# Splitting attention queries on their token rows and transposing once per head

## The reference

```python
def odd_mixer_latent(h, kc, vc, w_qkv, w_out, sink):
    q, k, v = split_qkv(h, w_qkv)          # 16 query heads of 64, 4 key/value heads
    q = rope_2d(q)
    k = rope_2d(k)
    return latent_attention(q, k, v, kc, vc, sink) @ w_out
...
    s_loc = jnp.einsum('bnqkgd,bnmkd->bnkgqm', qb, kw).astype(jnp.float32) * scale
    s_ctx = jnp.einsum('bnqkgd,bskd->bnkgqs', qb, kc).astype(jnp.float32) * scale
    p = jax.nn.softmax(jnp.concatenate([s_loc, s_ctx, sk], axis=-1), axis=-1)
```

## Time and profile before

| | us |
|---|---|
| median of three runs | 1598.37 |
| lowest and highest run | 1596.35, 1603.43 |
| profiled execution, its own time | 1597.03 |
| its span on the core | 1595.1 |
| TensorE busy | 1487.3 |
| VectorE busy | 667.9 |
| ScalarE busy | 545.9 |
| GpSimd busy | 508.8 |

### The profile page before, as it was taken

One profiled execution on the slowest core, in us unless ns is written; L12 is line 12 of the kernel. 1 busy time (PEld: TensorE's weight loads), 2 busy tenths in 40 slices (PEclk: granted clock), 3 DMA queues, 4 the chain that ended last, 5 costly groups with the idle time before them and its releaser, 6 DMA issues.

```text
span 1595.1 us, 20092 instructions
## 1 busy us (share of the span) xinstructions
PE 1487.3 (93%) x8338; PEld 1234.4 (77%) x8338; DVE 667.9 (42%) x1137; ACT 545.9 (34%) x904; POOL 508.8 (32%) x215
## 2 busy tenths in 40 slices
PE   4899889899999999999789889999799999999998
PEld 3776676688898899897567656657699889989985
DVE  4476763642222222233734566624532222223225
ACT  4376533631131232222531366515523113212311
POOL 1312133233143243232324234404333324332430
PEclk8999899999999999999999999999999999999999
DMA  9324145234343222134142000033332213212221
GB/s 343 126 80 132 60 130 180 67 121 158 124 139 113 73 84 75 55 104 157 45 172 80 27 1 2 1 107 131 99 100 80 76 57 101 64 61 93 80 84 75
DMA packets 90546, 153.87 MB, mean 96 GB/s; under 512 B 6404, under 2 KB 44752, under 8 KB 90456
## 3 DMA queue, kind: packets, MB, share of 16 engines
q1 hardware_dynamic: 82432, 145.76, 27.7%
q10 hardware_dynamic: 8024, 6.83, 1.5%
HBM read 149.69 MB, written 2.89 MB: 96 GB/s over the span
## 4 chain that ended last, share of the span: by engine, by line
PE 40%; DVE 3%; ACT 3%; DMA 2%; POOL 1%; issue 1%; ACTq 0%; DVEq 0%; SPq 0%
PE PS L1267 11%; PE PS L1268 11%; PE PS L1269 11%; PE PS L1556 2%; PE PS L1548 1%; POOL WL L927 1%; PE PS L1523 1%; PE PS L1506 1%; PE PS L1524 1%; DMA RAW<-in_w_ffn_in 1%; ACT WH L699 1%; DVE RAW L573 1%; PE PS L1319 1%; ACT RAW L573 1%; DMA RAW<-in_w_mod 0%
## 5 line engine op out<-in xcount | busy, mean ns | idle before, releaser
L927 POOL TENSOR_TENSOR WL<-RAW,WH 128x1024 fp32r<-128x1024 f32 x170 | 420.1, 2504 | 782.0 <-ACT WH L699 782.0
L1267 PE MATMUL PS<-HH,WH 128*128 128x384 f32 (+1 forms) x1152 | 359.6, 312 | 14.1 <-DVE HL L1080 7.9
L1268 PE MATMUL PS<-HL,WH 128*128 128x384 f32 (+1 forms) x1152 | 358.2, 311 | 0.0
L1269 PE MATMUL PS<-HH,WL 128*128 128x384 f32 (+1 forms) x1152 | 358.1, 311 | 0.0
L699 ACT CAST WH<-RAW 128x1024 fp32r<-128x1024 f32 x170 | 168.2, 1045 | 477.1 <-PE PS L1269 307.8
L1267 PE MATMUL PS<-WH,AH 128*128 128x512 f32 x640 | 251.4, 393 | 9.0 <-DVE ACC L1187 9.0
L1268 PE MATMUL PS<-WL,AH 128*128 128x512 f32 x640 | 250.1, 391 | 0.0
L1269 PE MATMUL PS<-WH,AL 128*128 128x512 f32 x640 | 250.0, 391 | 0.0
L1267 PEld LDWEIGHTS PS<-HH,WH 128*128 128x128 f32 x1152 | 221.1, 192 | 19.3 <-issue 10.2
L1268 PEld LDWEIGHTS PS<-HL,WH 128*128 128x128 f32 x1152 | 221.2, 192 | 0.6
L1269 PEld LDWEIGHTS PS<-HH,WL 128*128 128x128 f32 x1152 | 220.8, 192 | 0.0
(11 more groups left out here) (184 smaller groups left out, 1641.6 us busy)
## 6 DMA issues: line engine op xcount, KB each, us to landing
RAW<-in_w_mod SPq DMA_DIRECT2D x43, 1024.0 KB, 5.1
RAW<-in_w_ffn_in SPq DMA_DIRECT2D x32, 1024.0 KB, 5.7
RAW<-in_w_ffn_out SPq DMA_DIRECT2D x32, 1024.0 KB, 4.9
RAW<-in_w_in_even SPq DMA_DIRECT2D x7, 1024.0 KB, 5.5
RAW<-in_w_qkv SPq DMA_DIRECT2D x6, 1024.0 KB, 5.3
RAW<-in_w_out_even SPq DMA_DIRECT2D x4, 1024.0 KB, 5.1
RAW<-in_w_out_odd SPq DMA_DIRECT2D x4, 1024.0 KB, 6.2
X<-in_x_sample SPq DMA_DIRECT2D x4, 512.0 KB, 7.1
```

The costliest lines, as they stand in the source:

```text
L927: nc.gpsimd.tensor_tensor(ring_view(WL, ld, j), w_view(ld, b), ring_view(WH, ld, j).bitcast(f32), ALU.subtract).then_inc(w_lo, 1)
L1267: MM(out, wh, xh, start=first, stop=False)
L1268: MM(out, wh, xl, start=False, stop=False)
L1269: return MM(out, wl, xh, start=False, stop=last)
```

## The change

Before, TensorE makes both halves of `QS` by multiplying the query rows with the identity twice, into partitions 0 to 63 and 64 to 127 of a PSUM bank; ScalarE copies all of it, rounding; VectorE subtracts on the upper 64 partitions. After it, VectorE first makes rounded part and remainder side by side on the token rows, in one of two buffers (`Q2`, which share memory with `PART` and `BMR`), one unit ahead; TensorE transposes 128 columns per head at once, and ScalarE copies the bank to `QS` and frees it.

```diff
+        Q2B = alias("Q2B", [P, 512])
+        Q2 = [PART[:, :], Q2B[:, :]]
...
-                    nc.scalar.copy(QS[:, i % 2, :], m_bank(u)).then_inc(q_hi, 1)
+                    nc.scalar.copy(QS[:, i % 2, :], m_bank(u)).then_inc(m_free[u % 2], 1)
...
-            def query_remainder(i):
-
-                u = Q_M[i]
+            def query_split(i):
+
+                g, t = i % NKV, i // NKV
+                if i > 1:
+                    upto(dve, m_ready, Q_M[i - 2])
+                q = ACC[:, t, 256 * g:256 * g + 256].rearrange("p (h d) -> p h d", h=4)
+                hi, lo = (Q2[i % 2].rearrange("p (h w d) -> p h w d", h=4, w=2)[:, :, w, :] for w in (0, 1))
+                V_.tensor_copy(hi.bitcast(f32r), q).then_inc(q_hi, 1)
                 dve.wait_ge(q_hi, i + 1)
-                V_.tensor_tensor(QS[64:128, i % 2, :], m_bank(u)[64:128, :], QS[64:128, i % 2, :].bitcast(f32),
-                                 ALU.subtract).then_inc(m_free[u % 2], 1)
+                V_.tensor_tensor(lo, q, hi, ALU.subtract).then_inc(q_split, 1)
...
                 elif k == "Q":
                     if s["n"] == 0:
-                        query_remainder(0)
+                        upto(dve, b_free, QKV_B - LAT)
+                        query_split(0)
+                    if s["n"] + 1 == NKV:
+                        dve.wait_ge(qk_ready, 3 * LAT)
+                    if s["n"] < TT * NKV - 1:
+                        query_split(s["n"] + 1)
...
-                    if i + 1 < TT * NKV:
-                        query_remainder(i + 1)
...
                     m_acquire(u)
-                    if s["n"] == 0:
-                        upto(pe, b_free, QKV_B - LAT)
-                    if s["n"] == NKV:
-                        pe.wait_ge(qk_ready, 3 * LAT)
+                    pe.wait_ge(q_split, s["n"] + 1)
                     for h in range(4):
-                        c = HD * (4 * g + h)
-                        for half in (0, 64):
-                            ins = MM(m_bank(u)[half:half + 64, P * h:P * h + P], ACC[:, t, c:c + HD], IDN[:, :], start=True, stop=True)
+                        ins = TR(m_bank(u)[:, P * h:P * h + P], Q2[s["n"] % 2][:, P * h:P * h + P], IDN[:, :])
                     ins.then_inc(m_ready[u % 2], 1)
```

More of the change, by code:

```diff
@@ L475, in hybrid_step @@
         sum_ready = sem("sum_ready")
-        k_out, k_hi, q_hi = sem("k_out"), sem("k_hi"), sem("q_hi")
+        k_out, k_hi, q_hi, q_split = sem("k_out"), sem("k_hi"), sem("q_hi"), sem("q_split")
         qk_ready, v_done = sem("qk_ready"), sem("v_done")
```

## The result

| | before | after |
|---|---|---|
| median, us (4 runs each) | 1598.24 | 1588.84 |
| lowest and highest run | 1596.35, 1603.43 | 1587.29, 1591.47 |
| profiled execution, its own time | 1597.03 | 1587.29 |
| its span | 1595.1 | 1585.4 |

The ratio is 0.9932, with a 95% interval from 0.9912 to 0.9952: the changed kernel is 9.4 us faster by the medians. A second timing of the same kernel gave 0.9925 (0.9913 to 0.9937).

A forecast was written before the change was run, and what follows sets the result against it. TensorE was taken to set the pitch in the units of latent tiles. The terms 3.3 + 1.7 - 0.9 - 3.0 - 1.0 - 2.9 = -2.8 us took the median from 1598.37 to 1595.6 us, range 1590 to 1602.

The forecast's parts named there:

- The pair thus costs 0.38 + 0.69 + 0.08 ... = 1.15 us to 1.45 us: VectorE's new rounding copy and subtraction per unit, priced as 128x512 operations plus two hand-overs; 1.2 us taken.
- the first hole: At the first query, TensorE waits for VectorE's first split, so the projection goes on later: +3.3 us.
- units 7 to 11: Loop units where a GpSimd ring and the pair sticking out limit TensorE's saving: -1.0 us (0 to -2.15).
- The step falls from 1.02 to 0.59, by 0.43 us: TensorE's query step per unit: eight products of a 64-column weight tile become four transposes of 128 columns.
- units 12 to 18: TensorE-bound loop units with the pair covered: 7 x 0.43 less 0.1, -2.9 us.
- Units 2 to 6: Units 3 to 6, in a ring between ScalarE and VectorE, give -3.0 us; query 3 gives nothing.
- the remainder's place: VectorE's query remainder between sums and reduction, 0.72 us, goes away in units 3, 4, 5: 2.2 us.
- The ring of 7.64 us: Around unit 9, sums, GpSimd, small operations and exponentials form a cycle that an earlier reduction doesn't shorten.
- The half clock behind it: One stretch at granted clock 0.50 behind the first query's hole: +1.7 us (0 to 3.4).
- The saving without the stretch at the low clock: Rival: no low-clock stretch behind the first query's hole; sum -4.5, 1593.9 us; chance 0.22.
- VectorE does not become the bound: Denies the rival that a dear copy or GpSimd's hold-up makes VectorE the bound: +1.1, 1599.5 us; chance 0.20.
- The full promise: Rival: the whole 8.6 us saved on TensorE, first hole filled by something: about 1589.8 us; chance 0.07.

The follow-up runs named there:

- run 1: The kernel before with only TensorE's part: four full transposes of unsplit query rows for the eight identity products; 1589.64 us, ratio 0.9939.
- run 2: The changed kernel with only VectorE's split: TensorE makes eight 64-column products from the split rows instead of transposes; 1599.63 us, ratio 0.9995.
- run 3: The changed kernel with each query transpose issued a second time into the same place; 1595.58 us, ratio 0.9972.
- Run 5: The changed kernel with both operations of VectorE's split, copy and subtraction, issued twice; 1594.83 us, ratio 0.9977.
- run 4: The changed kernel with the first query's split ahead of the last rotary step of its projection group; 1584.49 us, timed again 1584.82.
- run 6: The changed kernel with GpSimd multiplying only the first half of each head's key columns by the inverse sum; 1587.31 us, ratio 0.9926.
- run 8: Run 4 with query transposes behind the first pair of weight transposes: 1586.31 us; also with per-head operations behind the maxima: 1581.69 us.

## Why the prediction was wrong

**What bounds the kernel: right.** TensorE's row set the pitch of the 4-key units before (8.68), and runs 1 to 3 move it by TensorE's work alone. Two prices of the sum were wrong.

**The step that failed first** is "The pair thus costs 0.38 + 0.69 + 0.08 ... = 1.15 us to 1.45 us", with both operations taken as 128 x 512. Four heads of 64 features are 256 values per row, and the order rows of the change say 128x4x64. The pair measured 0.28 + 0.42, with the hand-over 0.66, for the 1.2 taken. All that hung on it was too dear: the first hole (2.5 for 3.3, the smaller pair giving 0.5 of this) and "the pair sticks out by 0.3 to 0.6" in units 7 to 11. Run 5, whose pair is 1.44, takes 4.5 us more in the stage; since that pair is dearer than the 1.2 of the sum, this step's share of the 6.1 us by which the sum missed is less than these 4.5, and no run gives it more closely. The Trainium skill, VectorE: DVE Perf Modes, perf-mode tier table and errata section, would give (150 + 128) / 0.96 = 290 ns for the copy at its true size, by estimate; the trace has a median of 285.

**The second** is "The step falls from 1.02 to 0.59, by 0.43 us". The 0.59 was read up to the switch to value products, which doesn't follow a query step; between query and weight transposes it is 0.44. And 1.02 left out what the 64-column tile costs at its borders, 0.10 ahead of it and 0.06 behind. The saving is 0.73 per 4-key unit: run 3 splits it into 0.44 and 0.30. Over units 12 to 18 the four instructions give 3.1 us, as costed (3.0), and the tile 1.8 on top, which is nearly all of the miss there (2.0).

**Units 2 to 6** (-4.5 for -3.0). The forecast counted the remainder's place in units 3, 4 and 5 and left unit 2 out, where it gave 0.7: its pitch of 4.54 stays at 4.55 with the transposes alone (run 1) and falls to 3.79 with the split alone (run 2). Units 3 to 6 gave 3.8 in the first profile of the changed kernel and 3.1 in the second, so the 3.0 was near. The profile of before has half clock near 928; the first of after hasn't, the second has it near 931. How the 3.1 to 3.8 divide between split and transposes stays open.

**Units 7 to 11** (-2.4 for -1.0). The ring of 7.64 us is there as forecast: GpSimd's marks of units 8 and 9 lie 952.38 to 960.02 apart. But units 10 and 11, which took 7.95 and 8.58 before, fall to it. The pair takes nothing away there on balance: the transposes alone (run 1) give 1.9, with the split it is 2.4.

**The first query: right in place and mechanism**, and within 0.8 and 0.1 us in size; run 4 takes hole and clock away together and gains 4.4 us by the medians, and 3.6 when timed again. The half clock behind it was luck as much as reading: the forecast counted it in full with 1.7, and two of six profiles with this hole don't have it. The medians thus hold it in an unknown share of their runs.

**The rivals.** The saving without the stretch at the low clock said that where the hole falls is chance; the second profile of the changed kernel bears that out, but it is worth 1.6 us and doesn't carry the miss. VectorE does not become the bound (0.62 us of cover in the unit of the earlier trace rows), though it nearly does around unit 9, where the copies follow the pair at once. The clock doesn't fall inside the loop: it is 1.00 from 935 to 1035. The Trainium skill, TensorE: Matmul & The Clock Gate, Part 4 on PE-mode transpose, says that a transpose doesn't count as PE-busy in the same way; by that it might have fallen. No run here shows it: with each query transposed twice (run 3) the granted clock stays at 1.00 from 919.3 to 1120.7 us. The full promise at 1589.8 was the nearest in number, but its condition, a filled hole, wasn't met: the hole came, and the units gave more than the promise counted.

## What to carry to other kernels

Take the shape of a new operation from the order rows before choosing its price: a factor of two in one element count was the first cause of the miss, though the rows that gave the price were read rightly. Price an instruction on TensorE from the start of what stands before it to the start of what will stand behind it, and where the tile's width changes at its borders, look for a step without the change. When two engines hold a loop at nearly the same pitch, try the two edits together before dropping either: here each alone was below what the medians tell (0.9 and 1.1 us by the marks), and together they gave 3.1. And where a forecast counts on one stretch of half clock, profile the kernel twice: here it came in one profile and not in the other.

## What the runs showed of the hardware

- Eight products with a 64-column tile amid 128-column ones cost 0.30 us more per unit than eight of 128 columns (runs 2 and 3), at full clock.
- A VectorE operation with two tensor inputs in on-chip memory that starts beside a multiplication of GpSimd ends when that ends: in all 12 such units of the changed kernel the operation on 128 x 4 values ended 0.01 to 0.02 us behind GpSimd, after up to 1.19 us, and took 0.16 to 0.17 in the other 8. The split's copy, with one tensor input, was held too, once in that trace, at 909.48: 2314 ns against a median of 285, until 911.79, beside two GpSimd operations from 906.53 to 911.64. The per-head operations on 128 x 1 values were not held (0.58 us for four, wholly within GpSimd's work in run 8 at 950.48).
- After 3.05 us without work on TensorE the granted clock fell to half at 885.4, 1.5 us after work had begun again, for 3.4 us; a product then took 0.63 us instead of 0.39. After the same wait in the second profile of the changed kernel and in run 6 the clock stayed at 1.00.
